# Output projection of a decoder layer as seven half products with block sums

## The reference

```python
# Layer: x += W_out[concat(NSA heads, GLA heads)](RMSNorm(x) @ W_in); x += MoE(RMSNorm(x)).
D_MODEL = 1024; SEQ = 256; N_EXPERTS = 32; TOP_K = 4; D_FF = 1024
# o = concat(nsa (256 x 512), gla (256 x 512));  x1 = x + o @ w_out     (256x1024 @ 1024x1024)
def moe_ffn(h, w_router, b_router, ...):      # h = RMSNorm(x1)
    logits = xf @ w_router + b_router
    top_vals, top_idx = lax.top_k(logits, TOP_K)
    gate = jax.nn.softmax(top_vals, axis=-1)
    # each token goes through 4 of 32 experts: clamped_swiglu(x @ w_gate_up[e] + b) @ w_down[e]
```

## Time and profile before

| | us |
|---|---|
| median of 3 runs | 1066.3 |
| lowest, highest | 1064.62, 1068.13 |
| the profiled execution | 1063.68 |
| its span, first to last instruction | 1061.9 |
| TensorE busy | 1017.3 (96%) |
| VectorE, ScalarE, GpSimd busy | 294.1, 168.1, 15.9 |
| read from main memory | 424.83 MB |

### The profile page before, as it was taken

How to read it: one execution, slowest core, us unless ns; L and a number is a source line. 1 busy time by engine, 2 the same in 40 slices (tenths; PEclk the granted TensorE clock), 3 DMA queues, 4 the chain that set the end, 5 groups by cost and what they waited for, 6 DMA issues and landing times.

```text
span 1061.9 us, 12030 instructions
## 1 busy us (share of the span) xinstructions
PE 1017.3 (96%) x4977; PEld 410.7 (39%) x4977; DVE 294.1 (28%) x681; ACT 168.1 (16%) x324; POOL 15.9 (1%) x42
## 2 busy tenths in 40 slices
PE   9999999999999999999999999999999999989998
PEld 5555644333333333333333333333333333333334
DVE  1664625222222222211222122222112222221222
ACT  2434322111111111100111011111101111110111
POOL 4100000000000000000000000000000000000000
PEclk9999999999999999999999999999999999999999
DMA  9992668999999999999999999999999999999997
GB/s 296 362 408 88 246 270 343 426 425 436 428 430 433 433 433 430 428 430 431 434 434 433 433 426 430 433 432 434 432 431 426 426 434 433 434 431 430 420 426 276
DMA packets 36023, 426.45 MB, mean 402 GB/s; under 512 B 3782, under 2 KB 12062, under 8 KB 19728
## 3 DMA queue, kind: packets, MB, share of 16 engines
q1 hardware_dynamic: 33952, 424.52, 95.0%
q0 software_dynamic: 704, 1.04, 0.5%
q10 hardware_dynamic: 1328, 0.33, 0.1%
HBM read 424.83 MB, written 1.05 MB: 401 GB/s over the span
## 4 chain that ended last, share of the span: by engine, by line
PE 62%; DMA 34%; DVE 2%; SPq 1%; issue 1%; ACT 0%; DVEq 0%
DMA pair<-in_w_down 30%; PE bank L1741 24%; PE bank L1753 14%; PE bank L1329 5%; DMA pair<-in_w_gate_up 4%; PE bank L1775 4%; PE bank L1604 3%; PE bank L1725 2%; PE bank L1767 2%; PE bank L1733 1%; PE bank L1760 1%; PE bank L1401 1%; PE bank L1969 1%; SPq L369 1%; PE bank L1361 1%; PE bank L1388 1%
## 5 line engine op out<-in xcount | busy, mean ns | idle before, releaser
L1741 PE MATMUL bank<-pair,xs 128*64 128x512 f32 x2048 | 450.1, 594 | 21.0 <-DMA pair<-in_w_gate_up 19.9
L1741 PEld LDWEIGHTS bank<-pair,xs 128*64 128x64 f32 x2048 | 143.0, 137 | 323.1 <-issue 286.9
L1753 PE MATMUL bank<-pair,sig 128*64 128x512 f32 x960 | 212.2, 593 | 14.2 <-DMA pair<-in_w_down 14.2
L1222 DVE COPY gu<-bank 128x512 f32<-128x512 f32 x32 | 36.9, 1154 | 415.3 <-PE bank L1741 415.3
L1753 PEld LDWEIGHTS bank<-pair,sig 128*64 128x64 f32 x960 | 72.3, 137 | 149.9 <-issue 143.8
L760 ACT COPY gu<-bank 128x512 f32<-128x512 f32 x32 | 36.9, 1152 | 458.1 <-PE bank L1741 458.1
L862 DVE TENSOR_TENSOR xs<-bank,gt 128x512 f32<-128x512 f32 x31 | 21.4, 691 | 221.0 <-PE bank L1733 221.0
L1329 PE MATMUL bank<-stage,xt 128*128 128x512 f32 x160 | 72.2, 598 | 0.0
L1775 PE MATMUL bank<-ys,pgt 64*128 64x512 f32 x248 | 61.6, 615 | 0.3 <-ACT ys L765 0.3
L1725 PE MATMUL bank<-xr,onehot 128*64 128x512 f32 x248 | 58.5, 592 | 0.0
L765 ACT COPY ys<-bank 128x512 f32<-128x512 f32 x31 | 18.2, 586 | 206.9 <-PE bank L1753 206.9
(11 more groups left out here) (316 smaller groups left out, 496.8 us busy)
## 6 DMA issues: line engine op xcount, KB each, us to landing
pair<-in_w_gate_up SPq DMA_DIRECT2D x51, 4096.0 KB, 39.7
pair<-in_w_down SPq DMA_DIRECT2D x24, 4096.0 KB, 37.9
pair<-in_w_gate_up SPq DMA_DIRECT2D x22, 2048.0 KB, 14.7
pair<-in_w_down SPq DMA_DIRECT2D x15, 1024.0 KB, 13.3
pair<-in_w_down SPq DMA_DIRECT2D x6, 2048.0 KB, 33.0
stage<-in_w_in SPq DMA_DIRECT2D x5, 2048.0 KB, 19.2
pair<-in_w_gate_up SPq DMA_DIRECT2D x8, 1024.0 KB, 4.9
stage<-in_w_out SPq DMA_DIRECT2D x2, 2048.0 KB, 15.6
```

Of the source, the lines that this page charges most:

```text
L1222: V.tensor_copy(gu[:, 1, :].rearrange("p (i q) -> p q i", i=FQ), up_banks[1][:].rearrange("p (q i) -> p q i", i=FQ)).then_inc(s["gu_lo"], 1)
L1741: last = mm(up_banks[a][b * CAP:(b + 1) * CAP, :].rearrange("p (q i) -> p q i", i=FQ), xs[:, k, :], cols[:, b], start=k == 0, stop=k == DK ...
L1753: last = mm(down_bank[b * CAP:(b + 1) * CAP, :], actf[:, kk % FQ, kk // FQ, :], row[:, 512 * b:512 * (b + 1)], start=kk == 0, stop=kk == D ...
```

## The change

The output projection is cut in blocks of half the positions, half the features and half the columns. Before, each of the four output quarters is the sum of two half products, eight in all. After, there are seven, in Strassen's form (the variant with fewest sums). With o11, o21 the attention's features for tile 0 and 1, o12, o22 the GLA's, and w11 to w22 the blocks of w_out:

- GpSimd forms t3 = w22 - w12 (into w12's place), t2 = t3 + w11 (a place of its own, free after `grg`), t1 = w22 - t2 (into w11's place, after product 1) and t4 = t2 - w21 (into w12's place, after product 7), each in four instructions of 128x512.
- VectorE forms s3 = o11 - o21, s1 = o22 + o21, s2 = s1 - o11 and s4 = o12 - s2, each 128x512, and adds the products to x: twelve sums where there were four. Products 2 and 3 accumulate in the banks of 1 and 5.
- TensorE's order becomes product 1, product 7 with the transposes of `go` in it (tile 1 first), products 5, 6, 3, 2 and 4, with the turns and the router's matmuls between their k steps. The quarters are finished in the order (1,1), (1,0), (0,0), (0,1), written (m, ti).
- ScalarE copies o12 and o22, the second after s1, and loads the table of the square root then.
- Two of the three `busy` matmuls go.
- SyncE's transfers into pair 3 and extra2 wait for products 5, 6 (and all 16 weight sums), 3, 2 and 4.

```diff
-QUARTERS = [(0, 0), (1, 0), (0, 1), (1, 1)]
+QUARTERS = [(1, 1), (1, 0), (0, 0), (0, 1)]
+PRODUCTS = (1, 7, 5, 6, 3, 2, 4)
+BANK_OF = {1: 0, 2: 0, 3: 1, 5: 1, 4: 2, 7: 2, 6: 3}
...
+        def product_done(eng, n):
+            eng.wait_ge(s["wo_full"], PRODUCTS.index(n) + 1)
...
+        t1, t3, t4 = w11, w12, w12
...
-            sp.wait_ge(s["wo_low"], 1)
+            product_done(sp, 5)
             rows_in_place(3, 1, 1, 0, 1, "stage2")
-            sp.wait_ge(s["wo_low"], 2)
+            product_done(sp, 6)
+            sp.wait_ge(s["w_sum"], 16)
+            sp.dma_start(extra2[:], source(expert_behind(KEPT[1] - 1), 2)[:, SLOTW:]).then_inc(s["down1"], 16)
+            product_done(sp, 3)
+            rows_in_place(3, 1, 1, 3, 4, "ring3")
+            product_done(sp, 2)
+            rows_in_place(3, 1, 1, 1, 2, "stage2")
+            product_done(sp, 4)
             rows_in_place(3, 1, 1, 2, 3, "stage3")
...
+            def weight_sum(k, dst, a, b, op=ALU.subtract):
+                nc.gpsimd.tensor_tensor(dst[:, k, :], a[:, k, :], b[:, k, :], op).then_inc(s["w_sum"], 1)
+
+            front_arrived(pool, LOADS.index(("out", 0)))
+            front_arrived(pool, LOADS.index(("out", 1)))
+            for k in range(4):
+                weight_sum(k, t3, w22, w12)
+            pool.wait_ge(s["grg"], 1)
+            for k in range(4):
+                pool.wait_ge(s["w_sum"], k + 1)
+                weight_sum(k, t2, t3, w11, ALU.add)
+            product_done(pool, 1)
+            for k in range(4):
+                pool.wait_ge(s["w_sum"], 4 + k + 1)
+                weight_sum(k, t1, w22, t2)
+            product_done(pool, 7)
+            for k in range(4):
+                weight_sum(k, t4, t2, w21)
...
-            V.tensor_copy(ot[:, 0:4, P:S], banks[5][:].rearrange("p (k t) -> p k t", k=4)).then_inc(s["ot_late"], 1)
+            V.tensor_copy(o21, banks[5][:].rearrange("p (k t) -> p k t", k=4)).then_inc(s["o_sum"], 1)
+            dve.wait_ge(s["o_sum"], 1)
+            dve.wait_ge(s["ot"], 2)
+            V.tensor_tensor(s3[:], o11, o21, ALU.subtract).then_inc(s["o_sum"], 1)
...
+            dve.wait_ge(s["glaout"], NT)
+            dve.wait_ge(s["goT_full"], 1)
+            V.tensor_tensor(s1[:], banks[5][:].rearrange("p (k t) -> p k t", k=4), o21, ALU.add).then_inc(s["o_sum"], 1)
+            dve.wait_ge(s["o_sum"], 3)
+            V.tensor_tensor(s2[:], s1[:], o11, ALU.subtract).then_inc(s["o_sum"], 1)
...
+            c12 = add_part(1, 0, 1)
+            c21 = add_part(0, 1, 1)
+            c22 = add_part(1, 1, 1)
+            c21 = add_part(0, 1, 7, c21)
+            c22 = add_part(1, 1, 7, c22)
+            dve.wait_ge(s["ot_gla"], 1)
+            dve.wait_ge(s["o_sum"], 4)
+            V.tensor_tensor(s4[:], o12, s2[:], ALU.subtract).then_inc(s["o_sum"], 1)
+            c22 = add_part(1, 1, 5, c22)
+            residual(0, 6, c22)
+            c12 = add_part(1, 0, 6, c12)
+            c21 = add_part(0, 1, 6, c21)
+            half_square(1)
+            residual(1, 3, c12)
             half_square(0)
+            residual(2, 2, 0)
             root(0)
...
+            residual(3, 4, c21)
...
+            factors = {1: (o11, w11), 2: (o12, w21), 3: (s4, w22), 4: (o22, t4), 5: (s1, t1), 6: (s2, t2), 7: (s3, t3)}
...
+            pe.wait_ge(s["ot"], 1)
+            product(1, 0, 2)
+            pe.wait_ge(s["ot"], 2)
+            product(1, 2, 4)
+            pe.wait_ge(s["o_sum"], 2)
+            pe.wait_ge(s["w_sum"], 4)
+            product(7, 0, 3)
+            gla_turned(1, 1)
+            product(7, 3, 4)
+            gla_turned(0, 2)
+            pe.wait_ge(s["o_sum"], 3)
+            for k in range(4):
+                pe.wait_ge(s["w_sum"], 8 + k + 1)
+                product(5, k, k + 1)
+            pe.wait_ge(s["o_sum"], 4)
+            product(6)
+            pe.wait_ge(s["o_sum"], 5)
+            pe.wait_ge(s["x_part"], 6)
+            product(3)
...
+            rows_turned(0)
             pe.wait_ge(s["ot_gla"], 1)
+            product(2, 0, 2)
+            rows_turned(1)
+            product(2, 2, 4)
             pe.wait_ge(s["ot_gla"], 2)
+            pe.wait_ge(s["w_sum"], 16)
+            product(4, 0, 1)
+            route_parts(1)
+            product(4, 1, 2)
             rows_turned(2)
+            product(4, 2, 3)
+            route_parts(0).then_inc(s["rt_full"], 1)
+            product(4, 3, 4)
+            route(1, 4, DK)
             route_folded()
             rows_turned(3)
...
-            busy(1)
...
-            busy(1)
```

More of the change, by code:

```diff
@@ L1115, in _ @@
             dve.wait_ge(s["grg"], 1)
-            for ti in range(NT):
+            for ti in (1, 0):
                 for hp in range(2):
@@ L1597, in _, with product, gla_turned @@
             pe.wait_ge(s["oc_half"], 3)
-            def project_out(q, first, end):
-                m, ti = QUARTERS[q]
-                i = LOADS.index(("out", m))
-                front_arrived(pe, i)
+            factors = {1: (o11, w11), 2: (o12, w21), 3: (s4, w22), 4: (o22, t4), 5: (s1, t1), 6: (s2, t2), 7: (s3, t3)}
+            def product(n, first=0, end=4):
+                left, right = factors[n]
                 for k in range(first, end):
-                    last = mm(banks[2 * ti + m][:], ot[:, k, ti * P:(ti + 1) * P], front_slot(i)[:, k, :],
-                              start=k == 0, stop=k == DK - 1)
-                if end == DK:
+                    last = mm(banks[BANK_OF[n]][:], left[:, k, :], right[:, k, :], start=k == 0 and n not in (2, 3),
+                              stop=k == 3, skip_group_check=True)
+                if end == 4:
                     last.then_inc(s["wo_full"], 1)
-                elif q >= 2 and first == 0:
-                    last.then_inc(s["wo_low"], 1)
-            pe.wait_ge(s["ot"], 1)
-            project_out(0, 0, 2)
-            pe.wait_ge(s["ot"], 2)
-            project_out(0, 2, 4)
-            project_out(1, 0, 4)
-            pe.wait_ge(s["ot_late"], 1)
-            project_out(2, 0, 4)
-            project_out(3, 0, 4)
-            for ti in range(NT):
-                pe.wait_ge(s["glaout"], ti + 1)
+            def gla_turned(ti, told):
+                pe.wait_ge(s["glaout"], told)
                 for k in range(4):
@@ L1623, in _ @@
                 last.then_inc(s["goT_full"], 1)
+            for m in range(2):
+                front_arrived(pe, LOADS.index(("out", m)))
+            pe.wait_ge(s["ot"], 1)
[17 more added lines that the diff above has]
+            product(3)
             def rows_turned(q):
@@ L1644, in route_parts @@
                     last = mm(banks[4][E * g:E * (g + 1), P:2 * P], wrt[:, k, :], x1t[:, k, 0:P],
-                              start=half == 0, stop=half == 1)
+                              start=half == 1, stop=half == 0)
                 return last
@@ L1699, in first_turn @@
                     last = tp(first_banks[half][:, c * P:(c + 1) * P], cols[:, 2 * half + c, :], ident[:])
-                last.then_inc(s["xt_first"], 1)
+                last.then_inc(s["xt_full"], 1)
             pe.wait_ge(s["oh_first"], 1)
```

114 lines of the change are left out of this document (57 added, 57 removed).

## The result

| | before | after |
|---|---|---|
| median of 5 runs, side by side | 1066.37 us | 1071.16 us |
| lowest, highest | 1064.62, 1068.13 | 1070.15, 1071.73 |
| profiled execution, its span | 1063.68, 1061.9 | 1071.22, 1069.1 |
| product 1 (first matmul of the output projection) | 127.74 | 127.68 |
| first expert | 167.88 | 173.56 |

The changed kernel is slower by half a percent: ratio 1.0049, 95% interval 1.0033 to 1.0064. Forecast were 1063.2 us and a first expert at 164.8.

The account below looks back on a forecast made before the run. Weight transfers running without a gap fix the end, which moves with the first expert's start: 3.3 us earlier, less 0.25 us of VectorE delay, so 3.1 us less, from 1066.3 to 1063.2 us; range 1061.2 to 1065.2.

Parts of the forecast that it names:

- Two engines on one memory: GpSimd's t2 and t1 sums beside VectorE's norm chain: 0.25 us of delay taken, 6.0 us as the other bound.
- The rule of the sum: The end moves with the first expert's start, 167.88 us, if the transfer issued at 162.37 is in before the restart.
- Four k steps fewer, a wait removed, a turn moved: Output projection on TensorE: 3.45 us and a 0.33 us wait removed, 0.47 us added for a turn.
- Does VectorE keep up?: VectorE has go's second half and s1 ready when TensorE wants them, with 0.1 us to spare; costed at nothing.
- The GpSimd sums: GpSimd's weight sums take 1.2 us each and come in time for the products that need them; no wait.
- Rival 2: GpSimd sums come late for product 5 if over 1.5 us each; at 2.4 us a sum 1070.2 us; chance 0.08.
- The high bound: Each VectorE step reading two SBUF tensors, or a tensor_scalar, waits for a whole GpSimd sum: 6.0 us.
- After the last product: Routing from the last product to the first expert: choose(0) 2.8 us earlier, tile 1's reciprocal 3.0 us earlier.
- The 0.3 us credited for the two busy matmuls: Without them the position matmul no longer starts 0.2 us late and the first expert starts about 0.1 us earlier.
- The queue: The last weight transfer before the restart is in by 165.8 us, the restart comes at 166.6: 0.8 us margin.
- Rival 1: GpSimd sums hold VectorE up, transposes of go 6.0 us late, less 3.3: 2.7 us slower, 1069.0 us; chance 0.32.
- The clock: The prediction would be wrong altogether if TensorE's granted clock, 1.00, fell where the busy matmuls are gone; no size given.

Follow-up runs that it names:

- e5: e2 with one 256-column busy matmul where TensorE waits 0.68 us for ScalarE's copy of the last turned rows; 1060.90 us, ratio 0.9952.
- e12: The changed kernel with e9's busy matmul and 21 dummy matmuls ahead of the transposes of go; 1067.40 us, ratio 1.0024.
- e9: The changed kernel with one busy matmul where TensorE waited 0.68 us, ahead of tile 1's last routing; 1068.44 us, ratio 1.0029.
- e2: The changed kernel with one operand of each VectorE norm-chain step, and of s3, in PSUM; 1063.42 us, ratio 0.9989.
- e4: The kernel before without the two busy matmuls that the change removes; 1064.15 us, ratio 0.9996.
- e1: The changed kernel with its two removed busy matmuls back in their places; 1070.88 us, ratio 1.0055.
- e8: The changed kernel with t1's four GpSimd sums held until VectorE has finished go; 1066.98 us, ratio 1.0011.
- e3: e2 with the two removed busy matmuls back in their places; 1063.61 us, ratio 0.9988.
- e6: e5 with two more busy matmuls, ahead of the first gather and behind its tile 0; 1061.56 us, ratio 0.9956.

## Why the prediction was wrong, point by point

The step that failed is "Two engines on one memory": it put the meeting of the sums and the norm chain at 0.25 us, and it cost 5.41. Behind it stands a term that the sum did not have: the two falls of the clock, 4.27 us.

The path from product 1 to the first expert, taken apart by these kernels: 40.14 us before, 36.20 with chain and clock undisturbed (e5, -3.94), 41.61 with the blocked chain (e12, +5.41), 43.53 with the first fall (e9, +1.92), 45.88 with the second (+2.35).

- *The rule of the sum* (the end moves with the first expert and the restart) was right to within 0.9 us. The restart moved by +6.3 us and the span by +7.2; in e5 by -3.9 and -3.0.
- *Four k steps fewer, a wait removed, a turn moved*: right. From product 1 to the last residual e5 takes 27.71 us (155.48 - 127.77), before it was 31.17: -3.46 for the -3.31 of the sum.
- *Does VectorE keep up?* Right for a VectorE that nothing blocks: in e2 the go scaling starts at 132.15 and product 5 at 135.42, without a wait. The 0.1 us to spare was the warning, and "any delay of VectorE here is paid in full" is what happened.
- *The GpSimd sums*: right. 1.23 us each for 1.2, and in the changed kernel TensorE waits for none of them. Rival 2 had no part in it.
- *Two engines on one memory*: this step failed. I took 0.25 us from a copy beside a select at 31 us. The chain lost 0.52 (s3), 0.99 (first step) and four times 1.02 us, 5.6 in all, and TensorE 5.1 to 5.4. The high bound had the mechanism step by step and was 0.6 too large, mostly because it charged each step a whole sum, of which 0.17 is the step itself. (Its terms, 0.5 + 1.05 + 4 x 1.2, add up to 6.35, not to the 6.0 it gives.) The row was the nearest in shape, not in kind: a copy beside a select that reads one tensor, where the chain's steps stood beside sums that read two. That the copy has one input doesn't set it apart by itself, since three of the blocked steps have one. A row decides only for its own pair of instructions; without one of the right pair the two bounds should have been weighed the other way, or more evenly.
- *After the last product*: the order of the work was right (8.49 us from the last residual to the first expert in e5, 8.97 before), but the step left out what had covered ScalarE's copy of the last turned rows. That exposed 0.68 us, and through the clock this cost 2.35 to 2.58. The 0.3 us credited for the two busy matmuls was about right (e4: 0.48).
- *The queue*: right; in the window ahead of the restart the DMA share is 0.00, so the last fill was in. In e5, where the restart comes at 165.94, it is 0.09 from 165.5 to 166.0: in as well, but with under 0.5 us to spare, where 0.8 was forecast.
- *Rival 1* named the cause and gave 1069.0. At the first expert it had +2.7 us and +5.74 were measured: the two falls of the clock add 4.27, the chain's smaller price takes off 0.59 and the larger gain 0.64.
- *The clock*: the last sentence of the prediction named the event and the wrong cause, and the sum gave it no price. The first fall came while TensorE waited for go. The second came 2.6 us behind the wait of 0.68 us, near the place of the first busy matmul; but it came with that matmul too (e1), and not once the wait was filled (e9).

The side-by-side medians differ by 4.8 us and the two profiled executions by 7.5, since the profile of before is of an execution 2.7 us under its median. That profile has a clock of 1.00 throughout, but the kernel's executions beside these experiments have means of 0.994 to 1.00, so in some of them the clock falls too, where no profile shows it; beside e5 the medians differ by 4.4 us and the spans of the two profiles by 3.0. In the other four comparisons the kernel before has medians of 1064.75 to 1065.29.

Open remain: what the clock's fall depends on (waits of 1.06, 0.52 and 0.49 us among 512-column matmuls in e8 left it at 1.00, one of 0.68 among 32-column ones did not; e2 and e3, whose TensorE timelines agree up to there but for a shift of 0.05 us, fell at 158.7 and at 160.0), and why product 1 starts at different times in the profiles other than e6's.

## What to carry to other kernels

Before work goes to an idle GpSimd, list the VectorE instructions that will run beside it: a chain of tiny dependent steps with operands in SBUF loses one whole GpSimd instruction per step, and one operand of each in PSUM cost nothing here and cured it. Do so for every such chain that the work can meet when it comes early or late (e6), not only for the one in the profile. When matmuls are moved out from between a transpose and the use of its copy, look for the wait that they covered; in a thin stretch a wait well under 1 us can cost several times itself through the clock, and one dummy matmul in it, ahead of the fall, is worth trying. A small overlap seen in a trace bounds only the same pair of instruction kinds.

## What the runs showed of the hardware

- A blocked VectorE instruction starts in the record when it would have run, and its duration holds the wait (1.19 us for 0.17).
- Not only two-input steps: the one-input TENSOR_SCALAR of 128x8 in SBUF was blocked as well (1.16 and 1.19 us). A one-input RECIPROCAL of 128x8 beside t3's sums in e6 was not (0.19 us). The TENSOR_SCALARs on 47x1, beside t3's sums, were not, while two-input ones of that size were:

```profile
74.60 0.14 DVE L872 TENSOR_SCALAR st<-st 47x1 int32<-47x1 int32 x1
...
75.34 1.19 DVE L868 SCALAR_TENSOR_TENSOR st<-st 47x1 f32<-47x1 f32 x1
```

- Once fallen, the granted clock stayed at 0.50 for 6.8 us each time (137.3 to 144.2 and 168.0 to 174.9 us in the changed kernel, the same in e1, e2, e3, e8 and e9), although TensorE was busy again for most of it; only the early fall of e6 was shorter, 3.4 us.
